# A decoder layer on one core: the norm's factor spread by TensorE and applied before the token transposes, the first matmul unit in four stages

## The reference, cut to what matters

```
def rms_norm(x, g):
    xf = x.astype(jnp.float32)
    y = xf * lax.rsqrt(jnp.mean(xf * xf, axis=-1, keepdims=True) + RMS_EPS)
    return (y * g.astype(jnp.float32)).astype(x.dtype)

    h = rms_norm(x, g_mix)
    proj = h @ w_in
    q, k, v, u, gate_a, gate_s = jnp.split(proj, ...)
```

## Time and profile before

| | |
|---|---|
| time, median of 3 runs | 954.4 us (954.18 to 955.01) |
| the profiled execution | 953.97 us |
| its span | 952.2 us |
| TensorE matmul busy | 928.7 us, 98% of the span |
| TensorE weight load busy | 895.7 us, 94% |
| VectorE, ScalarE, GpSimd busy | 600.2, 433.8, 63.0 us |
| the first 28.1 us: TensorE busy | 15.9 us |

### The profile page before, as it was taken

How to read it: one execution, slowest core, us unless ns; L and a number is a source line. 1 busy time by engine, 2 the same in 40 slices (tenths; PEclk the granted TensorE clock), 3 DMA queues, 4 the chain that set the end, 5 groups by cost and what they waited for, 6 DMA issues and landing times.

```text
span 952.2 us, 17829 instructions
## 1 busy us (share of the span) xinstructions
PE 928.7 (98%) x7508; PEld 895.7 (94%) x7508; DVE 600.2 (63%) x820; ACT 433.8 (46%) x655; POOL 63.0 (7%) x111
## 2 busy tenths in 40 slices
PE   4999999999999999999999999999999999999998
PEld 4998899989999988999999999999999999999997
DVE  6498779921366644566567666666676666878453
ACT  6335333232577544454357344444444444445532
POOL 6000020410100310100000000000000000000000
PEclk8999999999999999999999999999999999999999
DMA  9522214742632739342322222332314332242203
GB/s 224 127 67 67 67 59 131 143 133 76 171 97 70 251 106 326 111 123 72 88 86 67 75 90 88 90 91 86 92 59 120 91 91 88 71 153 81 67 1 100
DMA packets 131015, 99.85 MB, mean 105 GB/s; under 512 B 15400, under 2 KB 121240, under 8 KB 130904
## 3 DMA queue, kind: packets, MB, share of 16 engines
q1 hardware_dynamic: 124392, 81.02, 29.0%
q0 software_dynamic: 5424, 17.65, 6.1%
q10 hardware_dynamic: 1120, 0.04, 0.1%
HBM read 87.53 MB, written 11.03 MB: 103 GB/s over the span
## 4 chain that ended last, share of the span: by engine, by line
PE 92%; ACT 3%; DVE 3%; issue 1%; DMA 1%; SPq 0%; ACTq 0%; DVEq 0%
PE dense L2144 63%; PE banks L2144 20%; PE scoreA L2144 4%; PE banks L2298 3%; PE scoreB L2144 1%; DMA xtok<-in_x_prompt 1%; ACT whi L1221 1%; ACT xsq L1359 0%; DVE mt L1676 0%; ACT ga L1548 0%; PE dense L2298 0%; DVE mt L1602 0%; DVE KTb L1909 0%; DVE sm L2027 0%; ACT act_hi L1370 0%
## 5 line engine op out<-in xcount | busy, mean ns | idle before, releaser
L1626 DVE TENSOR_TENSOR wlo<-wraw,whi 128x1024 fp32r<-128x1024 f32 (+1 forms) x139 | 148.6, 1072 | 104.1 <-ACT whi L1221 91.3
L2144 PE MATMUL dense<-hid,whi 128*128 128x256 f32 (+1 forms) x1024 | 176.1, 294 | 0.1
L2144 PE MATMUL dense<-act_hi,whi 128*128 128x256 f32 (+1 forms) x736 | 169.8, 301 | 1.0 <-DVE R L1704 1.0
L2144 PE MATMUL dense<-act_hi,wlo 128*128 128x256 f32 (+1 forms) x736 | 165.0, 295 | 0.0
L2144 PE MATMUL dense<-act_lo,whi 128*128 128x256 f32 (+1 forms) x736 | 164.4, 294 | 0.0
L2144 PEld LDWEIGHTS dense<-hid,whi 128*128 128x128 f32 x1024 | 152.4, 188 | 0.5 <-issue 0.5
L2144 PEld LDWEIGHTS dense<-act_hi,whi 128*128 128x128 f32 x736 | 124.3, 190 | 6.8 <-issue 4.9
L1221 ACT CAST whi<-wraw 128x1024 fp32r<-128x1024 f32 x100 | 104.8, 1049 | 46.5 <-PE banks L2144 44.5
L2144 PEld LDWEIGHTS dense<-act_hi,wlo 128*128 128x128 f32 x736 | 125.4, 189 | 0.0
L2144 PEld LDWEIGHTS dense<-act_lo,whi 128*128 128x128 f32 x736 | 124.5, 188 | 0.0
L2144 PE MATMUL dense<-hid,wlo 128*128 128x256 f32 (+1 forms) x512 | 109.0, 294 | 0.0
(11 more groups left out here) (342 smaller groups left out, 1566.4 us busy)
## 6 DMA issues: line engine op xcount, KB each, us to landing
wraw<-in_w_in SPq DMA_DIRECT2D x32, 512.0 KB, 4.4
wraw<-in_w_up SPq DMA_DIRECT2D x32, 512.0 KB, 4.0
wraw<-in_w_down SPq DMA_DIRECT2D x32, 512.0 KB, 3.8
gates_spill<-gst POOLq DMA_DIRECT2D x16, 288.0 KB, 2.4
page<-in_cache_k SPq DMA_DIRECT2D x16, 256.0 KB, 8.2
page<-in_cache_v SPq DMA_DIRECT2D x16, 256.0 KB, 7.0
wraw<-in_w_out SPq DMA_DIRECT2D x8, 512.0 KB, 4.1
wraw<-in_w_ple_gate SPq DMA_DIRECT2D x8, 512.0 KB, 4.0
```

Source lines behind the costliest of these rows:

```text
L1626: return nc.vector.tensor_tensor(out=lo, in0=whole, in1=f32(hi), op=ALU.subtract)
L2144: return nc.tensor.matmul(out, lhsT, rhs, start=start, stop=stop, skip_group_check=True)
```

## The change

**The factor.** g_mix is loaded as one row of 1024 numbers on one partition (`grow`). TensorE spreads it over 128 partitions: two matmuls of a row of ones with it (event `gmix`) fill PSUM slot 1 of `dense` (`gmix_rows`). The event `scale` now multiplies `xtok` by the token's value and by that row at once, with one scalar_tensor_tensor that reads PSUM. The multiplication behind the transposes and the buffer `hf` are gone: ScalarE casts `act_hi` out of the bank, and VectorE subtracts out of the bank too; a bank is free when `act_lo` has been computed. Tile 4 is transposed in one go, eight chunks of 64 columns into the bank of `dense` in which the row had been.

**The order.** `hlo` of tiles 0 and 1 stands ahead, and the first unit comes in four events `first`, between the transposes of the later tiles: 0: tokens 0 to 255 with whi, 1: the same with wlo, 2: the same tokens' `act_lo`, 3: tokens 256 to 575, all three sweeps.

```diff
@@ -218,30 +218,45 @@
             n[0] += 1
 
     def tokens(t):
-        for half in range(2):
-            event("h", t, half, place=(2 * t + half) % 4)
-
-    for t in range(3):
-        event("square", t)
-        event("scale", t)
+        for half in range(2 if t < 4 else 1):
+            event("h", t, half, place=(2 * t + half) % 4 if t < 4 else DENSE + 1)
+
+    event("gmix", place=DENSE + 1)
+    event("square", 0)
+    event("scale", 0)
+    event("square", 1)
+    event("scale", 1)
+    event("square", 2)
     tokens(0)
+    event("scale", 2)
     event("square", 3)
+    event("hlo", 0)
     tokens(1)
+    event("scale", 3)
+    event("hlo", 1)
     event("split_hi", 0)
     event("square", 4)
+    event("split_lo", 0)
     tokens(2)
-    event("scale", 3)
-    event("split_lo", 0)
+    dense_job(("m", 0, 0))
+    event("first", 0)
+    tokens(3)
     event("scale", 4)
-    tokens(3)
+    event("first", 1)
     tokens(4)
-    for t in range(5):
-        event("hlo", t)
+    event("first", 2)
+    event("hlo", 2)
+    event("hlo", 3)
+    event("hlo", 4)
+    event("first", 3)
     event("split", 1)
     event("split", 2)
     job("qs0", 0)
     job("qs1", 1)
-    unit()
+    flush()
+    event("unit", 0)
+    consumed(("split", 0))
+    n[0] += 1
     unit()
     event("qksum", 0)
     unit()
@@ -661 +675 @@
-        gains = sb("gains", [P, 3, KT])
+        gains = sb("gains", [P, 2, KT])
@@ -695 +709 @@
-        hf = placed(58880 + 24576, "hf", [P, 5, 2, 4, P])
+        grow = placed(58880 + 24576, "grow", [1, D])
@@ -817,6 +831,8 @@
         def prod(job):
 
             return product_of(jobs[job][0] - DENSE, 0, T)
+
+        gmix_rows = dense[:, 1].rearrange("p a n -> p (a n)")
 
@@ -1345 +1361 @@
            nc.scalar.preload_act_table_set("sqrt_and_others")
-            scalar.dma_start(gains[:, 0, :], i["g_mix"][0].rearrange("(k p) -> p k", p=P),
-                             allow_slow_non_contiguous=True).then_inc(gmix_in, 16)
+            scalar.dma_start(grow[:, :], i["g_mix"]).then_inc(gmix_in, 16)
@@ -1366,9 +1381,10 @@
                 elif k == "h":
                     t, half = a
                     t0, n = TOK[t]
-                    scalar.wait_ge(*read(("h", t, half)))
-                    nc.scalar.copy(act[0][:, 4 * half:4 * half + 4, t0:t0 + n], hf[:, t, half, :, 0:n]).then_inc(
-                        count.up(h_hi), 1)
+                    k0, nk = (4 * half, 4) if t < 4 else (0, KT)
+                    scalar.wait_ge(*full(e))
+                    nc.scalar.copy(act[0][:, k0:k0 + nk, t0:t0 + n],
+                                   bank(e).rearrange("p (k n) -> p k n", k=nk)).then_inc(count.up(h_hi), 1)
@@ -1749,25 +1765,21 @@
                     nc.vector.reciprocal(stat[0:n, 1, t:t + 1], stat[0:n, 0, t:t + 1]).then_inc(
                         count.up(dve_steps), 1)
                     vector.wait_ge(*count.last)
-                    nc.vector.tensor_scalar(xtok[0:n, t, :], xtok[0:n, t, :], stat[0:n, 1, t:t + 1], None,
-                                            ALU.mult).then_inc(count.up(xn_ready), 1)
-                elif k == "h":
-                    t, half = a
-                    t0, n = TOK[t]
-                    vector.wait_ge(*full(e))
                     if t == 0:
-                        vector.wait_ge(gmix_in, 16)
-                    nc.vector.tensor_tensor(out=hf[:, t, half, :, 0:n],
-                                               in0=gains[:, 0, 4 * half:4 * half + 4].unsqueeze(2).to_broadcast([P, 4, n]),
-                                               in1=bank(e).rearrange("p (k n) -> p k n", k=4)[:, :, 0:n], op=ALU.mult).then_inc(
-                                                   count.upto(*read(e)), 1)
+                        vector.wait_ge(*full("gmix"))
+                    ins = nc.vector.scalar_tensor_tensor(out=xtok[0:n, t, :], in0=xtok[0:n, t, :],
+                                                         scalar=stat[0:n, 1, t:t + 1], in1=gmix_rows[0:n, :],
+                                                         op0=ALU.mult, op1=ALU.mult)
+                    ins.then_inc(count.up(xn_ready) if t < 4 else count.upto(*read("gmix")), 1)
                 elif k == "hlo":
                     t = a[0]
                     t0, n = TOK[t]
-                    for half in range(2):
+                    for half in range(2 if t < 4 else 1):
+                        k0, nk = (4 * half, 4) if t < 4 else (0, KT)
+                        turned = ("h", t, half)
                         vector.wait_ge(h_hi, 2 * t + half + 1)
-                        lower(act[1][:, 4 * half:4 * half + 4, t0:t0 + n], hf[:, t, half, :, 0:n],
-                              act[0][:, 4 * half:4 * half + 4, t0:t0 + n]).then_inc(count.up(h_lo), 1)
+                        lower(act[1][:, k0:k0 + nk, t0:t0 + n], bank(turned).rearrange("p (k n) -> p k n", k=nk),
+                              act[0][:, k0:k0 + nk, t0:t0 + n]).then_inc(count.upto(*read(turned)), 1)
@@ -2163,7 +2175,7 @@
                     return pT
                 return act
 
-            def first_unit():
+            def first_unit(stage):
 
                 slot = jobs["m", 0, 0][0] - DENSE
                 wh, wl = [wview(w, 0, 0) for w in (whi, wlo)]
@@ -2175,16 +2187,22 @@
                                  start=start and k == 0, stop=stop and k == KT - 1)
                     return ins
 
-                tensor.wait_ge(h_hi, 4)
-                sweep(0, wh, act[0], start=True)
-                sweep(0, wl, act[0])
-                tensor.wait_ge(h_hi, 10)
-                sweep(1, wh, act[0], start=True)
-                sweep(1, wl, act[0])
-                tensor.wait_ge(h_lo, 4)
-                sweep(0, wh, act[1], stop=True)
-                tensor.wait_ge(h_lo, 10)
-                sweep(1, wh, act[1], stop=True).then_inc(full_of(("m", 0, 0)), 1)
+                if stage == 0:
+                    tensor.wait_ge(w_hi, turn["split", 0])
+                    tensor.wait_ge(h_hi, 4)
+                    sweep(0, wh, act[0], start=True)
+                elif stage == 1:
+                    tensor.wait_ge(w_lo, turn["split", 0])
+                    sweep(0, wl, act[0])
+                elif stage == 2:
+                    tensor.wait_ge(*read(("h", 1, 1)))
+                    sweep(0, wh, act[1], stop=True)
+                else:
+                    tensor.wait_ge(h_hi, 9)
+                    sweep(1, wh, act[0], start=True)
+                    sweep(1, wl, act[0])
+                    tensor.wait_ge(*read(("h", 4, 0)))
+                    sweep(1, wh, act[1], stop=True).then_inc(full_of(("m", 0, 0)), 1)
 
@@ -2211,14 +2229,13 @@
             begun = {}
 
             def unit(u, js=None, k0=0, k1=None):
+                if u == 0:
+                    return
                 kind, m0, nk, nm = units[u]
                 k1 = k1 or nk
                 if k0 == 0:
                     tensor.wait_ge(w_lo, turn["split", u])
                 x = operand(u)
-                if u == 0:
-                    first_unit()
-                    return
@@ -2312,18 +2329,27 @@
 
             for e in schedule:
                 k, a = e[0], e[1:]
-                if k == "h":
+                if k == "gmix":
+                    tensor.wait_ge(ident_ready, 1)
+                    tensor.wait_ge(gmix_in, 16)
+                    for half in range(2):
+                        c = slice(BANK * half, BANK * half + BANK)
+                        ins = mm(gmix_rows[:, c], ones[0:1, :], grow[0:1, c], True, True)
+                    ins.then_inc(full_of(k), 1)
+                elif k == "h":
                     t, half = a
                     n = TOK[t][1]
-                    if t == 0 and half == 0:
-                        tensor.wait_ge(ident_ready, 1)
-                    tensor.wait_ge(xn_ready, t + 1)
+                    k0, nk = (4 * half, 4) if t < 4 else (0, KT)
+                    if t < 4:
+                        tensor.wait_ge(xn_ready, t + 1)
                     if used_before(e):
                         tensor.wait_ge(*free(e))
-                    for c in range(4):
-                        c0 = P * (4 * half + c)
-                        ins = transpose(bank(e)[:, P * c:P * c + n], xtok[0:n, t, c0:c0 + P], n)
+                    for c in range(nk):
+                        c0 = P * (k0 + c)
+                        ins = transpose(bank(e)[:, n * c:n * c + n], xtok[0:n, t, c0:c0 + P], n)
                     ins.then_inc(full_of(e), 1)
+                elif k == "first":
+                    first_unit(a[0])
```

More of the change, by code:

```diff
@@ L553, in build @@
         h_hi = semaphore("h_hi")
-        h_lo = semaphore("h_lo")
         w_hi = semaphore("w_hi")
@@ L1240, in feed @@
                 scalar.wait_ge(*read(job))
-                nc.scalar.activation(act[0][:, m, :], R[:, m, :], ACT.Copy, scale=gains[:, w, m:m + 1]).then_inc(
```

(7 more changed lines are left out.)

## The result

The changed kernel takes 955.78 us (median of 15 runs, 955.42 to 963.85), the kernel before 954.67 (15 runs, 954.07 to 959.99). The ratio is 1.0023, with a 95% interval of 1.0013 to 1.0033. The forecast was 949.6, in a range of 948.2 to 952.3: wrong in value and in sign. The profiled execution of the changed kernel took 955.48 us, 1.51 more than that of before (953.97).

The account below looks back on a forecast made before the run. TensorE, busy 98% of the span, bounds the kernel; its opening has waits and low clock. Gains of 0.75 (tokens), 3.8 (TensorE) and 0.3 (load) sum to 4.85 us: 954.4 becomes 949.6, range 948.2 to 952.3.

Parts of the forecast that it names:

- Behind unit 0: From unit 1 to the end: all follows TensorE's list, so the opening's gain stays; 0 us taken as given back.
- The token side: Opening, ScalarE and VectorE up to tile 4's scale: done at 18.25 instead of 18.99, a gain of 0.75 us.
- The load term: ScalarE's queue at the start: without g_mix's 1024 pieces x lands sooner; 0.3 us taken, between 0 and 0.99.
- The new scale: VectorE's scaling of each token tile, now reading PSUM: 1.28 us against 0.74 to 0.81, bounds 1.22 and 1.55.
- The low halves out of PSUM: VectorE's subtractions reading a bank instead of SBUF: nothing charged for reading PSUM, bounds 0 and 0.3 us.
- rival E: Part of the gain given back at the parameter loads, or first weight late: 1 to 2 us, 951 to 952; chance 0.07.
- The TensorE side: TensorE work behind tile 4's scale before unit 1: 5.25 us in place of 9.05, a gain of 3.8 us.
- The row: Spreading g_mix's row by float32 matmuls takes 2.4 us, landing at 3 to 4.5, ready between 5.4 and 6.9; cost 0.
- D: Rival: the row lands at 5.95, shifting the chain by 0.9 us, and no load gain: 950.8 us; chance 0.07.
- A: Rival: clock falls once more in the opening, low over `first` 1, tile 4, half of `first` 2: 1.6 us, 951.2; chance 0.16.
- B: Rival: clock stays low in the opening until `first` 3; unit 1 at 27.3, gain 0.8 us, 953.6; chance 0.09.
- C: Rival: clock stays low through `first` 3 too; unit 1 at 30.8, 2.7 us later than before, 957.1; chance 0.05.

Follow-up runs that it names:

- experiment 2: Changed kernel plus an unused 64-byte tensor per partition in front of the activations; 950.99 us median, ratio 0.9961 to the kernel before.
- experiment 10: Changed kernel plus a 64-byte spacer and the old g_mix load in 1024 pieces, issued behind the row's load; 951.29 us median, ratio 0.9951 to the kernel before.
- experiment 1: Changed kernel plus an unused 32-byte tensor per partition in front of the activations; 951.91 us median, ratio 0.996 to the kernel before.
- 7: Changed kernel plus 32 bytes in front of the weights and 32 behind the small tiles; 953.44 us median, ratio 0.9966 to the kernel before.
- 11: Changed kernel plus a 64-byte spacer, first weight tile loaded ahead of the last token tile; 950.92 us median, ratio 0.9943 to the kernel before.
- experiment 12: Changed kernel plus a 64-byte spacer and two overwritten 256-column float32 matmuls (the filler) before the first sweep; 948.96 us median, ratio 0.9939 to the kernel before.
- experiment 3: Kernel before with g_mix's factor in its own tile and `gains` cut to two rows, same instructions; 965.81 us median, ratio 1.0111 to the kernel before.

## Why the prediction was wrong, step by step

**The step that failed** is "*Behind unit 0.* Everything follows TensorE's list, and the weights are loaded when slots become free, so the gain stays", and with it the sentence "nothing in this change makes a matmul faster; it can only remove waits". It held for waits, queues and slots. It left out that a change can alter a matmul's pace, and the edit that did, `gains` with two rows instead of three, had no term in the sum. It cost 7.24 us, against all the terms of the sum together, 4.85. At a good distance the same step holds to 0.04 us (924.14 against 924.10, experiment 2), and the forecast of 949.1 for the profiled execution came within 0.4 of 948.68. The median there, 950.99, is 1.4 above the forecast and inside the range.

**The token side** was to gain 0.75 and the load 0.3. Tile 4's transposes begin at 17.15 in place of 19.05: 1.90. The load term was mis-sized: the square of tile 1 began at 6.04 with no wait, so it was at its upper bound, 1.0 (that it was g_mix's load which had held it up is not shown, experiment 10). ScalarE and VectorE in the changed kernel:

```profile
6.04 1.06 ACT L1374 ACTIVATE xsq<-xtok 128x1024 f32<-128x1024 f32 x1
9.18 1.05 ACT L1386 CAST act_hi<-banks 128x512 fp32r<-128x512 f32 x2
12.99 1.05 ACT L1237 CAST whi<-wraw 128x1024 fp32r<-128x1024 f32 x1 [0.22 <-DMA wraw<-in_w_in]
```
```profile
6.20 1.28 DVE L1770 SCALAR_TENSOR_TENSOR xtok<-xtok,stat,dense 128x1024 f32<-128x1024 f32 x1
13.29 1.28 DVE L1642 TENSOR_TENSOR act_lo<-banks,act_hi 128x512 fp32r<-128x512 f32 x2
15.82 1.27 DVE L1770 SCALAR_TENSOR_TENSOR xtok<-xtok,stat,dense 64x1024 f32<-64x1024 f32 x1
```

The new scale takes 1.28 us, as worked out. The first cast came at 9.18, not 10.1: here too the earlier x. From then on the steps are those of the working, each about 1.1 us earlier (tile 4 scaled at 17.09, not 18.25). The casts out of PSUM take 1.05 a pair where 1.2 was taken. The low halves out of PSUM take 678 ns each, 676 out of SBUF before: nothing charged, nothing found. The Trainium skill, VectorE: DVE Perf Modes, section on the TRN2 errata, gives the operation out of PSUM 62 cycles more, an estimate of 65 ns; these 2 ns don't show it. The first weight came 0.22 late, the beginning of rival E.

**The TensorE side** was to gain 3.8: from tile 4's transposes to unit 1 it is 22.36 - 17.15 = 5.21 in place of 9.05, so 3.84. The clock was at its high level from sweep 0 on in this execution. That it comes out to 0.04 us is partly luck: the transposes cost 0.64 in place of 0.8, and the 256 sweep 1.05 in place of 0.93.

**The row** took 3.75 us and not 2.4. Width and clock were scaled rightly, but not the row that the estimate rests on the earlier trace rows: the trace has its four records in two pairs, started at 34.49 and 34.50 and at 34.74 and 34.75 us, so that 0.67 us held only two steps of 0.25 and not four. The row's four came one behind another, 0.85 to 0.98 us apart. By 0.25 x 512/288 x 2 = 0.89 for each the four would have made 3.6, near what was measured. The row ended at 6.09, just ahead of 6.20, since it landed at 2.34 and not at 3 to 4.5; two errors met, and D did not come in this execution. In nine of the twelve other profiled executions that spread the row, tile 0's scale did wait for it, 0.19 to 0.61 us.

**Rivals.** A was given 16 in 100 and 1.6 us. It is absent in the changed kernel's profile. At the good distances three of the four profiled executions without the filler show it: against unit 1 at 22.76 in experiment 2, it came at 25.93 in experiment 1, 24.29 in 7 and 23.85 in 11, so 3.2, 1.5 and 1.1 us later. Of the 3.2, 0.6 were there before sweep 0 (begun at 15.07 and not at 14.48). In two of the three the price was about right; the chance was too low.

B and C did not come in the changed kernel's profile: sweep 0 cost 1.05 us (14.09 to 15.14), the high level. Before it the level was low. The sixteen transposes of tiles 0 and 1 took 3.68 us and the eight of tile 2 1.94, the pace of the low level. So it rose while TensorE, since the row's end at 6.09, had done nothing but transposes. The Trainium skill, TensorE: Matmul & The Clock Gate, Part 4, says that transposes don't count as work for the gate; by that the level would have stayed low for sweep 0. The trace does not agree, by those 1.05 us. Most of B did come in the profiled execution of experiment 10, low through sweep 0, tile 3's transposes and the larger part of sweep 1, with unit 1 at 24.82. Against the 5% for slower, the kernel was slower, by a mechanism that none of the rivals had.

## What to carry to other kernels

Read every edit of a tile's shape as a shift of all tiles declared behind it. TensorE's pace here hung on the distance between weights and activations (of the four remainders modulo 128 that were tried, 32 and 64 good, 0 and 96 bad, 0.8% of the whole time), so pin that distance, or compare the pace of a long uniform stretch before and after, ahead of any story about the edited part. And where the granted clock can fall behind an idle stretch, count it into the price of that stretch.

## What was not expected of the hardware

- 96 dense matmuls (256 and 320 columns in turn) in 12.59, 12.64, 12.80 or 12.82 us at granted clock 1.00, by that distance alone; 84 of 288 columns in 11.20, 11.11, 11.16 or 11.11, in another order of the four. Whether the weights' read meets the moving read, and which of `whi` and `wlo` matters, stays open.
- A float32 matmul appears as two records. The row's, with an operand on one partition and 512 columns, start 0.85 us apart (the first two 0.98) at the low level; the filler's in experiment 12, with 128 partitions and 256 columns, 0.22 apart at the high one. Twice the columns and half the clock make 0.22 to 0.86, so the one partition costs nothing that shows. The 288-column records on 16 output rows ran in pairs, 7 ns apart.
- Whether the clock falls isn't fixed by the program: one kernel gave 948.4 and 953.5 us on one chip. It fell behind 0.82 us without a matmul near 212 us in experiment 3, and did not at the same place before the change, behind the same 0.82. What decides it stays open.
- In the three profiled kernels that issue 1024 pieces of four bytes first, at 0.85 us, the square of tile 1 waits 0.82 to 0.99 us for its 512 KB of x. It does not wait where one row takes their place, nor where the pieces follow the row 0.56 us later. That the pieces cause the wait is argued, not shown.
